# A PEER layer on one core: 33 of 192 expert dots made as GpSimd products and ScalarE sums, with picks and one-hot groups placed anew

## The reference, cut to what matters

```python
q = (xt @ w_q).reshape(n, PEER_HEADS, 2, PEER_QDIM // 2)
s = jnp.einsum("nhpd,hpkd->nhpk", q, sub_keys)
s1, i1 = lax.top_k(s[:, :, 0], PEER_TOPK)
s2, i2 = lax.top_k(s[:, :, 1], PEER_TOPK)
cand_s = s1[..., :, None] + s2[..., None, :]
...
top_s, pos = lax.top_k(cand_s, PEER_TOPK)
g = jax.nn.softmax(top_s, axis=-1)
a = gelu(einsum("td,thkd->thk", xc, u_tab[experts]))
out = einsum("thk,thkd->td", g * a, v_tab[experts])
```

## Time and profile before

| | us |
|---|---|
| median of three runs | 2150.76 (2142.43 to 2152.95) |
| profiled execution, its own time | 2148.01 |
| its span | 2146.7 |
| first dot of unit 0 starts | 784.93 |
| last dot's successor on DVE starts | 1365.82 |
| first matmul of the V blocks | 1406.04 |
| busy over the span | PE 77%, DVE 74%, ACT 39%, POOL 19% |

### The profile page before, as it was taken

The page is one execution under the profiler, slowest core; times in us unless marked ns, Lnnn a source line. Parts: engine busy times, 40 slices in busy tenths (PEclk is TensorE's granted clock), DMA queues, the critical chain, the costliest instruction groups (busy, mean ns, idle before and its releaser), DMA issues.

```text
span 2146.7 us, 25780 instructions
## 1 busy us (share of the span) xinstructions
PE 1663.2 (77%) x9820; PEld 1470.7 (69%) x9820; DVE 1594.6 (74%) x2019; ACT 833.5 (39%) x1336; POOL 413.8 (19%) x386
## 2 busy tenths in 40 slices
PE   7999999999999899500000333599999999999996
PEld 6999999999998787400000222478877888888884
DVE  5464444444565459799999999977888888888888
ACT  5444444444343321000002988343433343443432
POOL 0000000010151013333333222011221212212221
PEclk9999999999999999855555555799999999999998
DMA  9555555555468479899999888468999999999995
GB/s 315 157 169 167 167 166 169 171 170 161 144 190 309 143 302 416 348 413 376 381 383 363 316 313 311 170 252 324 415 394 366 397 374 378 375 382 377 361 392 216
DMA packets 293529, 627.67 MB, mean 292 GB/s; under 512 B 10364, under 2 KB 223405, under 8 KB 234958
## 3 DMA queue, kind: packets, MB, share of 16 engines
q0 software_dynamic: 48400, 343.95, 41.2%
q1 hardware_dynamic: 244558, 282.20, 38.7%
q10 hardware_dynamic: 496, 0.58, 0.1%
HBM read 622.45 MB, written 8.44 MB: 294 GB/s over the span
## 4 chain that ended last, share of the span: by engine, by line
PE 68%; DVE 20%; DVEq 5%; issue 3%; DMA 2%; ACT 1%; POOL 1%; SPq 0%; POOLq 0%; ACTq 0%
PE ps L1598 32%; PE ps L1329 22%; DVE u_ring L1208 13%; PE ps L1511 5%; PE ps L1489 4%; DVEq L1164 4%; PE ps L1574 1%; PE ps L1434 1%; DMA v_raw<-in_peer_v 1%; PE ps L1415 1%; DVE ones L1235 1%; PE ps L1424 0%; PE ps L1515 0%; POOL msum L548 0%; DVE pick L1194 0%
## 5 line engine op out<-in xcount | busy, mean ns | idle before, releaser
L986 DVE TENSOR_TENSOR w_lo<-raw,w_hi 128x2048 fp32r<-128x2048 f32 x112 | 259.1, 2313 | 330.8 <-ACT w_hi L589 330.7
L1329 PE MATMUL ps<-act_hi,w_hi 128*128 128x256 f32 x1536 | 441.6, 288 | 4.8 <-DVE act_lo L1111 2.9
L1208 DVE CUSTOM_DVE_ANT_0 u_ring<-u_ring,ps 128x2048 f32<-128x2048 f32 x192 | 433.1, 2279 | 14.5 <-DMA u_ring<-in_peer_u,idx_all 14.3
L1329 PE MATMUL ps<-act_hi,w_lo 128*128 128x256 f32 x1536 | 435.8, 284 | 0.0
L1329 PE MATMUL ps<-act_lo,w_hi 128*128 128x256 f32 x1536 | 435.7, 284 | 0.0
L924 ACT ACTIVATE v_hi<-v_raw 128x2048 fp32r<-128x2048 f32 x128 | 245.4, 1917 | 430.8 <-PE ps L1598 414.0
L1598 PE MATMUL ps<-v_hi,c_hi 128*128 128x512 f32 x1024 | 407.1, 398 | 4.1 <-DVE c_lo L1291 4.1
L1598 PE MATMUL ps<-v_hi,c_lo 128*128 128x512 f32 x1024 | 405.2, 396 | 0.0
L1598 PE MATMUL ps<-v_lo,c_hi 128*128 128x512 f32 x1024 | 402.5, 393 | 0.0
L1289 DVE TENSOR_TENSOR v_lo<-v_raw,v_hi 128x2048 fp32r<-128x2048 f32 x128 | 293.6, 2294 | 90.6 <-ACT v_hi L924 90.3
L589 ACT ACTIVATE w_hi<-raw 128x2048 fp32r<-128x2048 f32 x112 | 214.1, 1911 | 265.2 <-PE ps L1329 220.6
(11 more groups left out here) (210 smaller groups left out, 2045.9 us busy)
## 6 DMA issues: line engine op xcount, KB each, us to landing
v_raw<-in_peer_v SPq DMA_DIRECT2D x128, 1024.0 KB, 7.4
raw<-in_w_in SPq DMA_DIRECT2D x80, 1024.0 KB
raw<-in_w_out SPq DMA_DIRECT2D x16, 1024.0 KB
wq_raw<-in_peer_w_q SPq DMA_DIRECT2D x8, 2048.0 KB, 18.1
raw<-in_w_br_a SPq DMA_DIRECT2D x16, 512.0 KB
bias_by_query<-bias_by_distance POOLq DMA_DIRECT2D x1, 4096.0 KB, 20.1
bias_st<-bias_by_query POOLq DMA_DIRECT2D x16, 256.0 KB, 4.6
raw<-in_w_br_b SPq DMA_DIRECT2D x16, 256.0 KB
```

The source lines that it names most:

```text
L986: nc.vector.tensor_tensor(w_lo[:, j % NHL], raw[:, j % NRAW], w_hi[:, j % NHL].bitcast(F32), ALU.subtract).then_inc(lo_done, 1)
L1208: nc.vector.tensor_tensor_reduce(out=u_ring[:, k % RING_U], in0=u_ring[:, k % RING_U], in1=h2p[u // PH], scale=0.5, scalar=0.0, op0=ALU.mu ...
L1329: last = nc.tensor.matmul(out_ap, w_parts[wp][:, slot, k], act_parts[ap][:, k], start=(k == k0 and m == 0), stop=(k == k1 - 1 and m == 2))
```

## The change

**Dots.** 33 of the 192 early dots leave DVE: three in each of units 2 to 7 (picks 3, 8, 13, with pick 3 of unit 2 excepted) and four in each of units 8 to 11 (picks 2, 6, 10, 13). For such a pair POOL multiplies the slot by `h2` in SBUF, in four instructions of 128x512, and ACT sums the slot with one 128x2048 activation that accumulates. POOL does the product of the pair six places back in the list, after each gather. The gather that takes the slot next waits for ACT's sum.

**Picks.** `PICK_PLAN` hands out the 195 steps of units 1 to 15: 13 in unit 0, 16 in unit 1, then one or two behind every DVE dot until they run out in unit 10 (21, 20, 19, 20, 19, 20 in units 2 to 7; 18, 18, 11, 0 in units 8 to 11). Before, it was 13 steps in each of units 0 to 7 and 11, and 26 in each of units 8 to 10.

**One-hot groups.** ACT has 18 of tile 0's groups, at fixed (unit, pick) places, and DVE 14, in tiles of their own (`ones_d`): 2, 2, 4 and 6 in units 8 to 11. None is left behind the last dot except the 16 late groups.

**Gates.** In the projection loop, `squared(0)` moves to `w == 8`, `tanh_of(0)` to 11, `squared(1)` to 13, `exps_of(2)` from 11 to 10, and `exps_of(3)` comes in at 14.

```diff
-ACT_GROUPS = 28
+ACT_GROUP_AT = {(8, 3): 0, (8, 5): 1, (8, 8): 2, (8, 11): 3, (8, 14): 4, (9, 1): 5, (9, 4): 6, (9, 7): 7, (9, 10): 8, (9, 13): 9,
...
+DVE_GROUP_AT = {(8, 9): 0, (8, 14): 1, (9, 5): 2, (9, 12): 3, (10, 3): 4, (10, 7): 5, (10, 11): 6, (10, 14): 7,
...
+AHEAD = 6
+def on_pool(u, k):
+    return u >= 2 and k in ((3, 8, 13) if u < PH else (2, 6, 10, 13)) and (u, k) != (2, 3)
...
+        if u == 0:
+            count = 2 if 3 <= k < 9 else 1 if k == 9 else 0
+        elif u == 1:
+            count = 1
+        else:
+            count = 0 if on_pool(u, k) else 1 + dve_dots(u, k) % 2
...
+        def products(u, k):
+            pool.wait_ge(u_in[k % RING_U], u_count(u, k))
+            for c in range(NWIDE):
+                cols = u_ring[:, k % RING_U, WIDE * c:WIDE * c + WIDE]
+                last = nc.gpsimd.tensor_tensor(cols, cols, h2[:, u // PH, WIDE * c:WIDE * c + WIDE], ALU.mult)
+            last.then_inc(prod_ok, 1)
...
+                before = EARLY[n - (RING if u < 2 else RING_U)]
+                if on_pool(*before):
+                    pool.wait_ge(sum_dot, pool_dots(*before))
+                else:
+                    pool.wait_ge(dot_ok, dve_dots(*before))
+            gather(u_ring[:, k % RING_U], u_tab, u, k).then_inc(u_in[k % RING_U], 16)
+            if n >= AHEAD and on_pool(*EARLY[n - AHEAD]):
+                products(*EARLY[n - AHEAD])
...
+            if w == 8:
+                squared(0)
+            if w == 10:
                 exps_of(2)
                 scores_of(3)
+            if w == 11:
+                tanh_of(0)
             if w == 13:
-                squared(0)
-                tanh_of(0)
+                squared(1)
...
+        def sum_of(u, k):
+            act.wait_ge(prod_ok, pool_dots(u, k))
+            slot = u_ring[:, k % RING_U]
+            nc.scalar.activation(slot, slot, ACT.Copy, scale=0.5, accum_out=early_dots[:, u, k:k + 1]).then_inc(sum_dot, 1)
...
+            if k >= 2 and on_pool(c, k - 2):
+                sum_of(c, k - 2)
+            if (c, k) in ACT_GROUP_AT:
+                one_hots(ACT_GROUP_AT[c, k])
+            if DVE_GROUP_AT.get((c, k), 0):
+                dve_group_out(DVE_GROUP_AT[c, k] - 1)
...
+        for c, k in EARLY:
...
+            if not on_pool(c, k):
                 dot(c, k)
...
+            for u, step in PICK_PLAN[c, k]:
+                pick_step(u, step)
+            if (c, k) in DVE_GROUP_AT:
+                j = DVE_GROUP_AT[c, k]
+                dve.wait_ge(pk_ev, 1)
+                wait(dve, dc_pe, j - 1)
+                one_hots(ones_d[:, 0, j % 2], ones_d[:, 1, j % 2], GTOK * (ACT_GROUPS + j)).then_inc(od_ok, 1)
```

More of the change, by code:

```diff
@@ L102, with dve_dots, pool_dots, pick_plan @@
     OPS_AT[b].append(n)
+EARLY = [(u, k) for u in range(N_EARLY) for k in range(PTOP)]
+AHEAD = 6
+def on_pool(u, k):
+    return u >= 2 and k in ((3, 8, 13) if u < PH else (2, 6, 10, 13)) and (u, k) != (2, 3)
+def dve_dots(u, k):
+    return sum(1 for at in EARLY if at <= (u, k) and not on_pool(*at))
+def pool_dots(u, k):
+    return sum(1 for at in EARLY if at <= (u, k) and on_pool(*at))
+EARLY_DOTS = dve_dots(N_EARLY, 0)
+def pick_plan():
+    plan, done = {}, PICK_STEPS
+    for n, (u, k) in enumerate(EARLY):
+        if u == 0:
[4 more added lines that the diff above has]
+            count = 0 if on_pool(u, k) else 1 + dve_dots(u, k) % 2
+        count = min(count, NU * PICK_STEPS - done)
+        plan[u, k] = [divmod(done + m, PICK_STEPS) for m in range(count)]
+        done += count
+    return plan
+PICK_PLAN = pick_plan()
+assert sum(len(steps) for steps in PICK_PLAN.values()) == (NU - 1) * PICK_STEPS
 def bucket_onehots():
@@ L339, in build @@
     oh_ok = sem("oh_ok")
-    oh_dve = sem("oh_dve")
+    od_ok = sem("od_ok")
+    late_oh = sem("late_oh")
+    dc_pe = sem("dc_pe")
+    dc_ev = sem("dc_ev")
+    prod_ok = sem("prod_ok")
+    sum_dot = sem("sum_dot")
     c_pe = sem("c_pe")
@@ L889, in one_hots @@
             last.then_inc(oh_ok, 1)
[L891 to L913, removed]
-                if first + 1 < NU:
-                    scores_of(first + 1)
-            if q == per_phase - 1 and first + 1 < NU:
-                exps_of(first + 1)
-                scores_of(first + 2)
+        for c, k in EARLY[2 * PTOP:]:
+            if k == 0:
+                if c == 4:
+                    act.wait_ge(s2_ev, 2 * PH)
+                    nc.scalar.activation(h2p[1], h2[:, 1], ACT.Copy).then_inc(hp_ok, 1)
+                if c > 2:
+                    squared(c - 1)
+                if c == PH:
+                    tanh_of(c - 1)
+                    picks_turned(0)
+            if c != PH and k == (9 if c < PH else 5):
+                tanh_of(c - 1)
+            for u, step in PICK_PLAN[c, k]:
+                if step == 7 and u > 3:
+                    exps_of(u)
+                    if u + 1 < NU:
+                        scores_of(u + 1)
+            if k >= 2 and on_pool(c, k - 2):
[4 more added lines that the diff above has]
+                dve_group_out(DVE_GROUP_AT[c, k] - 1)
         matrices(ACT_GROUPS - 1)
+        dve_group_out(DVE_GROUPS - 1)
+        act.wait_ge(dc_pe, DVE_GROUPS)
         def high_v(b):
```

123 lines of the change are left out of this document (62 added, 61 removed).

## The result

The changed kernel took 2172.87 us (median of five runs, one of them disturbed and 95 us longer; the ratio leaves that one out), the kernel before 2149.0 us (five runs). The ratio is 1.0105, 95% interval 1.0087 to 1.0122: **1% slower**, where 2121 us was forecast. The profiled execution took 2172.87 us, its span is 2171.6 us.

The account below looks back on a forecast made before the run. DVE was taken as the bound, transfers close behind. Unit 1 -8.9, units 2 to 7 +1.4, units 8 to 11 -18.1, tail -3.1 gave -28.7 us, forecast 2121 us, range 2083 to 2152.

Parts of the forecast that it names:

- An operation that falls into a piece waits half of it, 0.62.: Units 2 to 7: a two-SBUF-input DVE operation falling into a 1.25 us POOL product piece loses 0.62 us, 10.6 us together.
- POOL is inside a product for 0.31 of the time: Units 2 to 7: POOL multiplies 85 of 272 us, taken as hit chance for some 55 two-input DVE operations.
- the sum: DVE's losses to POOL's products, units 2 to 11: small operations 10.6 and 11 us, group multiplications 12.6; forecast as 34.
- The forecast sign of it: In the profile after, DVE's two-tile pick operations would have means up by 0.2 us, 0.69 to 0.9.
- The tail's "I add 1 us": Behind the last dot: 1 us added to the late groups because PE did less ahead of them; tail net -3.
- unit 1: Unit 1: earlier squared(0) ends DVE's 11.65 us standstill; with 1.5 us for data waits, -8.9 us.
- DVE's own work in units 2 to 7: Units 2 to 7: 79 dots, 119 steps and gates take DVE 259.6 us, against 268.9 before.
- transfers and POOL not binding: Units 2 to 11: DMA transfers would not bind (rival at 2109, chance 0.17); POOL hidden early, DVE's equal in units 8 to 11.
- POOL's waits: POOL's waits for slots would fall from 381 us to under 100, with some 25 us new for ACT's sums.
- The first, no collisions: Rival: products fall beside dots and POOL is never late; near 2083 us, chance 0.13.
- The third: Rival: a waiting POOL takes the port after each DVE operation, every hit waits a whole piece; 2159 us, chance 0.17.
- The fourth: Rival: dots hold the port too, so each POOL piece waits for a dot; +218 us, 2366, chance 0.06.

Follow-up runs that it names:

- Experiment 2: The changed kernel with POOL waiting on a semaphore after each of a product's four pieces before issuing the next; 2132.16 us (one run).
- Experiment 5: The changed kernel with the gate steps of units 2 to 7 moved behind dots 5 and 10, tanh_of to place 6; 2150.70 us (one run).
- Experiment 6: The changed kernel steered: one-instruction products pinned to dots, port-using DVE work kept out of them, 29 dots moved; 2105.61 us, ratio 0.9804.
- experiment 4: The kernel before with only unit 0's gates moved, squared(0) to block 8 and tanh_of(0) to block 11; 2136.45 us, ratio 0.9943.
- experiment 1: The changed kernel with each product as one 128x2048 POOL instruction in place of four of 128x512; 2156.76 us (one run).
- experiment 8: Experiment 6's kernel with 44 extra unused PE matmuls ahead of the turning of the late picks; 2107.69 us, ratio 0.9828.
- experiment 10: Experiment 6's kernel with 32 extra unused matmuls ahead of the turning and ACT's two V-block splits moved behind its tanh; 2103.04 us, ratio 0.9805.

## Why the prediction was wrong

1. **"An operation that falls into a piece waits half of it, 0.62."** This step failed, and it decides the sign. The piece was taken as what holds the port, after rows 10, where POOL's addition has nothing close behind it. The runs show that POOL's four pieces hold it as one, and the gather ahead of them too if they follow it without a pause: the operations that were caught in units 2 to 7 waited 1.8 to 2.7 us each, to the end of the product's 4.9, and those of units 8 to 11 up to 8.2. Experiment 2 shows that it is the missing gap that does this. All together: 34 us of losses forecast, 88 measured, against 62.7 saved.
2. **"POOL is inside a product for 0.31 of the time"**, used as the chance of each of 55 operations (0.45 for those of units 8 to 11). The share itself was right (17 x 4.92 of 289 us, 0.29), but the places are fixed, and so are the victims: `coef` of units 2 to 7 was hit six times of six, `pick` and `cand` there in none of 28 executions. Added up the chance came out too high. Of what the sum counted, it expected 17, 18 and 6 hits (small operations of units 2 to 7, of 8 to 11 with the first halves, and multiplications), and there were 9, 10 and 3. This error worked against the first: with as many hits as forecast the loss would have been larger. Experiments 5 and 6 show the places in both directions. The forecast sign of it, pick operations on two tiles with means up from 0.69 to 0.9, is absent in units 2 to 7: 0.69.
3. **What the sum left out.** That a TENSOR_SCALAR with one SBUF tensor needs the port was right for the groups, and their four multiplications lost 15.7 us where 12.6 were forecast. But the same holds for `thl`, with 16 integers a partition, which the sum did not count at all: 13 us in units 2 to 7, the larger part of the 19 by which they missed. The first halves of the groups lost 18.4 us where 14 x 0.45 x 0.62 = 4 were forecast: that is step 1 again.
4. **The tail's "I add 1 us"** for a PE at 0.50: 4.2 us measured, so the tail gained nothing. The late groups did begin as forecast.
5. Right: unit 1 (-8.9, measured -9.0, and -11.3 for the whole kernel in experiment 4); DVE's own work in units 2 to 7 (259.6 forecast, 261.2 when steered); dots free of the port; the products' and sums' own durations (4.92 and 2.1 us); transfers and POOL not binding. POOL's waits were only half right: for slots they fell from 381 to 150 us, not under 100, and for ACT's sums they were 77 and not 25, at no cost since DVE was busy.
6. **The rivals.** The first, no collisions, is what steering brings (2083 forecast for 33 dots; 2098 to 2106 with 29). The third had the right point of decision, losses over 64 us, and for its groups the right price, "the whole product", but for single operations one piece; its 2159 was the nearest of all to 2173. It should have been carried to its end: a lock that is released only when the other side pauses. The range ended at 2152, below even that rival's own time. That 2159 came near is in part luck: its hits were too many and its wait too short. The fourth misread its evidence: the gather of 3.06 us in rows 11 lay beside the subtraction of a V block (128x2048, 2.29 us, both inputs in SBUF), not beside a dot.

The Trainium skill says (SBUF — State Buffer, "Who interferes with whom") that whoever issues first gets the pair for the whole instruction. The runs here agree for one instruction (experiment 1), and show more for several that follow without a pause.

## What to carry to other kernels

Work moved to GpSimd is priced by what it holds, not by what it takes: add up the whole run of its instructions without a pause, a gather directly ahead included, and look which VectorE operations with a second SBUF tensor, or a scalar multiplication of an SBUF tensor, stand inside it, however small they are. In a program with fixed order this is a matter of places and not of chances; so pin each GpSimd product to dots by a semaphore and keep such operations out, or at least let GpSimd wait between pieces. And before counting what a TensorE stretch behind an idle time takes, look at the granted clock at which it was measured.

## What the hardware showed unexpectedly

- Four 128x512 products on GpSimd, issued back to back, made a VectorE operation of 0.17 us take 2.79 us, past two of their boundaries. With a semaphore wait between them the product took 5.30 us instead of 4.92, and the same operation 0.35 us on average instead of 1.64.
- Eight of them in a row, two products, made a 0.69 us operation take 8.86 us.
- A product that follows a gather without a pause held off VectorE operations that had begun during the gather, 0.14 to 0.64 us before its end (5.2 to 5.7 us each, six times); beside gathers with no product behind them such operations took at most 0.13 us more than alone.
- The other way round, gathers that began 0.18 us into a VectorE `pick` operation of 0.69 us with two SBUF inputs took 1.33 us instead of 0.94 in the kernel before.
- A TENSOR_SCALAR of 128x16 uint32 with one SBUF input is held in the same way (1.64 us against 0.175). FIND_INDEX8, MAX8, MATCH_REPLACE8, RECIPROCAL and the dot with its second input in PSUM, which fell into the same products, took their usual times.
- A product of 128x2048 took 4.52 us in one instruction and 4.92 us in four.
- PE's granted clock fell from 1.00 to 0.50 behind 4.3 us of near idleness in experiment 8, and behind 2.7 us without a matmul in experiment 10, and stayed there for some 24 and 14 us of matmuls with few pauses. With the hole filled it did not fall.
